# Triangular inversion of the recurrent tiles: the 4x4 blocks by a square and one product, the square copied by ScalarE

## What is computed

```
def step(state, inp):
    r_t, w_t, k_t, v_t, kk_t, a_t = inp
    sa = jnp.einsum('bhij,bhj->bhi', state, -kk_t)
    state = (state * w_t[:, :, None, :] + sa[..., None] * (kk_t * a_t)[:, :, None, :]
             + v_t[..., None] * k_t[:, :, None, :])
    return state, jnp.einsum('bhij,bhj->bhi', state, r_t)
```

## Time and profile before

| | |
|---|---|
| three runs | 1869.55, 1875.81, 1876.41 us |
| median | 1875.81 us |
| profiled execution, span from first to last instruction | 1869.1 us |
| `mix`, eight tiles | some 560 us |
| TensorE busy | 87% |
| VectorE busy | 50% |
| ScalarE busy | 30% |
| GpSimd busy | 20% |

### The profile page before, as it was taken

How to read it: one execution, slowest core, us unless ns; L and a number is a source line. 1 busy time by engine, 2 the same in 40 slices (tenths; PEclk the granted TensorE clock), 3 DMA queues, 4 the chain that set the end, 5 groups by cost and what they waited for, 6 DMA issues and landing times. The chain is left out here.

```text
span 1869.1 us, 40718 instructions
## 1 busy us (share of the span) xinstructions
PE 1629.8 (87%) x16070; PEld 1075.9 (58%) x16071; DVE 937.1 (50%) x2046; ACT 559.8 (30%) x1099; POOL 369.4 (20%) x825
## 2 busy tenths in 40 slices
PE   4999999876788889888886898498999999999976
PEld 2744444336666667676664455365666666666652
DVE  4257686346768777768562224432233333333326
ACT  4115887723334434434332112010111111111121
POOL 7301457701101100101000000111111111111110
PEclk8999999988899999999997999599999999999997
DMA  9513434320013011000002563599999799978735
GB/s 332 164 60 150 162 127 167 121 86 27 13 28 106 14 38 28 13 28 18 19 8 75 192 218 137 224 352 408 405 398 366 285 385 388 366 294 313 285 138 230
DMA packets 131649, 334.88 MB, mean 179 GB/s; under 512 B 14174, under 2 KB 52110, under 8 KB 130497
## 3 DMA queue, kind: packets, MB, share of 16 engines
q1 hardware_dynamic: 122496, 314.12, 44.6%
q0 software_dynamic: 9024, 19.00, 3.5%
HBM read 303.23 MB, written 38.82 MB: 183 GB/s over the span
## 5 line engine op out<-in xcount | busy, mean ns | idle before, releaser
L2043 PE MATMUL psX<-arena 128*64 128x256 f32 x1536 | 180.0, 388 | 14.2 <-DMA arena<-in_e_down_dram 12.6
L2067 PE MATMUL psP<-arena 128*64 128x512 f32 x768 | 175.4, 599 | 0.0
L2043 PEld LDWEIGHTS psX<-arena 128*64 128x64 f32 x1536 | 115.2, 140 | 91.4 <-issue 43.5
L806 PE MATMUL psP<-arena 128*128 128x512 f32 x320 | 141.1, 595 | 4.4 <-DVE arena L712 2.9
L506 ACT ACTIVATE arena<-arena 128x1024 bf16<-128x1024 f32 (+5 forms) x138 | 134.2, 973 | 32.5 <-POOL arena L464 28.6
L806 PE MATMUL psX<-arena 128*128 128x512 f32 x320 | 140.9, 595 | 3.4 <-DVE arena L712 1.9
L1740 PE MATMUL psP<-arena 128*128 128x512 f32 x256 | 116.4, 613 | 9.8 <-PEq L112 4.6
L1918 ACT ACTIVATE arena<-arena 64x1024 f32<-64x1024 f32 x49 | 51.7, 1055 | 237.9 <-PE psT L2029 210.9
L1927 ACT ACTIVATE arena<-psX 128x256 f32<-128x256 f32 x48 | 18.4, 383 | 317.3 <-PE psX L2043 317.3
L1261 PE MATMUL psP<-ckvT,arena 128*128 128x512 f32 (+3 forms) x192 | 79.4, 524 | 33.2 <-DVE st L1100 22.0
L806 PEld LDWEIGHTS psP<-arena 128*128 128x128 f32 x320 | 59.9, 190 | 81.4 <-issue 75.4
(11 more groups left out here) (413 smaller groups left out, 2870.0 us busy)
## 6 DMA issues: line engine op xcount, KB each, us to landing
arena<-in_e_gate_dram SPq DMA_DIRECT2D x32, 2048.0 KB, 9.5
arena<-in_e_up_dram SPq DMA_DIRECT2D x32, 2048.0 KB, 15.2
arena<-in_e_down_dram SPq DMA_DIRECT2D x32, 2048.0 KB, 9.4
arena<-in_ada_w_dram SPq DMA_DIRECT2D x12, 2048.0 KB, 16.4
proj_T<-arena SPq DMA_DIRECT2D x36, 256.0 KB, 2.0
arena<-in_x_dram SPq DMA_DIRECT2D x16, 512.0 KB, 5.7
arena<-in_w_in_dram SPq DMA_DIRECT2D x4, 2048.0 KB, 8.4
arena<-in_final_ada_w_dram SPq DMA_DIRECT2D x4, 2048.0 KB, 12.3
```

Source lines behind the costliest of these rows:

```text
L806: mm = pe.matmul(psum[b], w[:, k, first:first + P], hT[:, k, 512 * half:512 * half + 512], start=(k == 0), stop=(k == KD - 1))
L2043: mm = pe.matmul(psum["X0"][BLK * h:BLK * h + BLK, 0:DE // 2], xT[:, k, :], gate_w[u][:, k, DE // 2 * h:DE // 2 * (h + 1)], start=(k == 0) ...
L2067: mm = pe.matmul(psum["P0"][BLK * half:BLK * half + BLK, :], hidT[:, f, h, :], down_w[u][:, KE // 2 * h + f, D // 2 * half:D // 2 * (half ...
```

## The change

Level 0 and level 1 become one step on the 4x4 diagonal blocks. With N4 the part of N inside the 4x4 blocks, N4 to the fourth power is zero, so the inverse of (I - N4) is (I + N4)(I + N4 N4).

- Constants: `m_lvl[0]` becomes the upper mask of the 4x4 blocks (levels 0 and 1 added), `m_first` the lower one. Six more rows on GpSimd behind the `steps` constants.
- VectorE writes `low4` = N4 (plain) from PSUM in place of `AA`, then `high4` = N4 transposed into TT[0] with no identity, then `AA`, which is wanted from level 2 on only. The identity is added to TT[0] behind the X of level 1, where VectorE masked X before.
- TensorE makes X of level 1 from `low4` and TT[0]: the square of N4. It needs no mask, and ScalarE copies it to `Xs`. The products W and the addition L1214 stay as they are.
- GpSimd writes TT[1] with one addition, `low4` plus identity, in place of a mask and an addition.
- One more buffer, `low4`, of 512 columns.

```diff
@@ -450,6 +450,9 @@
                     step(pool.memset(halves[:, i:i + 1], -float(2.0 ** -(i + 1))))
                 for i in range(SEQ // BLK - 1):
                     step(pool.memset(steps[:, i:i + 1], float(BLK * (i + 1))))
+                step(pool.tensor_tensor(m_lvl[:, 0, :], m_lvl[:, 0, :], m_lvl[:, 1, :], ALU.add))
+                both_chunks(m_lvl[:, 1, :], lambda: merge(2, False))
+                step(pool.tensor_tensor(m_first[:, :], m_first[:, :], m_lvl[:, 1, :], ALU.add))
                 step(pool.memset(Z[:, :, :, :], 0.0))
                 pool.wait_ge(*at("kv_var", 0))
                 link(pool, pool.tensor_tensor(kv_rs, kv_var, mhalf[:, 0:2 * NT], ALU.pow), "kv_rs", 0)
@@ -849,6 +852,7 @@
             mixT, qlT, olT = A.take(KD, P), A.take(NH, P), A.take(NH, P)
             lg = A.take(2, SEQ)
             PT = A.take(NT, 2, P)
+            low4 = A.take(2, NPAIR, CHUNK)

             s_mx, s_gn, s_kk = st[:, 40:48], st[:, 48:72], st[:, 72:88]
             s_bon = (st[:, 24:32], st[:, 32:40])
@@ -943,10 +947,8 @@
                     ends = dx.rearrange("p (q c) i -> p c q i", c=2)[:, :, :, CHUNK:].to_broadcast([P, 2, NPAIR, CHUNK])
                     spread = ident64[:, :].unsqueeze(1).unsqueeze(1).to_broadcast([P, 2, NPAIR, CHUNK])
                     link(pool, pool.tensor_tensor(decI, ends, spread, ALU.mult), "dec_i", t)
-                    pool.wait_ge(*at("aa", t, 1))
-                    T0 = TT[:, :, 1, :, :]
-                    step(pool.tensor_tensor(T0, AA, m_first[:, :].unsqueeze(1).unsqueeze(1).to_broadcast([P, 2, NPAIR, CHUNK]), ALU.mult))
-                    link(pool, pool.tensor_tensor(T0, T0, spread, ALU.add), "t_first", t)
+                    pool.wait_ge(*at("low4", t, 1))
+                    link(pool, pool.tensor_tensor(TT[:, :, 1, :, :], low4, spread, ALU.add), "t_first", t)
                     if t:
                         output_roots(t - 1)
                     if t + 1 < NT:
@@ -1043,6 +1045,9 @@
                     for l in range(1, LEVELS):
                         next(turns, None)
                         if l == 1:
+                            for g in range(2):
+                                act.wait_ge(*at("x_done", t, l, g))
+                                link(act, act.activation(Xs[:, g], by_q(f"X{g}", CHUNK), ACT.Copy), "square", t, g)
                             act.wait_ge(*at("a_turned", t))
                             link(act, act.activation(R[:, :, :, 0, :], psum["T1"].rearrange("p (q g i) -> p q g i", q=NPAIR, g=2), ACT.Copy), "a_rows", t)
                             act.wait_ge(*at("av_done", t))
@@ -1186,10 +1191,11 @@
                         dve.wait_ge(*at("aa_done", t))
                         if t:
                             dve.wait_ge(*at("t_first", t - 1))
+                        link(dve, dve.tensor_tensor(low4[:, g], by_q(f"W{g}", CHUNK), each(m_first[:, :], NPAIR), ALU.mult), "low4", t, g)
+                    Tt0 = TT[:, :, 0, :, :]
+                    link(dve, dve.tensor_tensor(Tt0, AbB[:, :, :, 0, :], m_lvl[:, 0, :].unsqueeze(1).unsqueeze(1).to_broadcast([P, 2, NPAIR, CHUNK]), ALU.mult), "high4", t)
+                    for g in range(2):
                         link(dve, dve.tensor_tensor(AA[:, g], by_q(f"W{g}", CHUNK), each(m_low[:, :], NPAIR), ALU.mult), "aa", t, g)
-                    Tt0 = TT[:, :, 0, :, :]
-                    step(dve.tensor_tensor(Tt0, AbB[:, :, :, 0, :], m_lvl[:, 0, :].unsqueeze(1).unsqueeze(1).to_broadcast([P, 2, NPAIR, CHUNK]), ALU.mult))
-                    link(dve, dve.tensor_tensor(Tt0, Tt0, ident64[:, :].unsqueeze(1).unsqueeze(1).to_broadcast([P, 2, NPAIR, CHUNK]), ALU.add), "tt", t, 0)
                     if t:
                         centre(t - 1)
                     next(turns, None)
@@ -1200,9 +1206,13 @@
                     next(tail, None)
                     whole = dx[:, :, CHUNK:CHUNK + 1].to_broadcast([P, NH, CHUNK])
                     for l in range(1, LEVELS):
-                        for g in range(2):
-                            dve.wait_ge(*at("x_done", t, l, g))
-                            link(dve, dve.tensor_tensor(Xs[:, g], by_q(f"X{g}", CHUNK), each(m_lvl[:, l, :], NPAIR), ALU.mult), "xs", t, l, g)
+                        if l == 1:
+                            dve.wait_ge(*at("x_done", t, l, 1))
+                            step(dve.tensor_tensor(Tt0, Tt0, ident64[:, :].unsqueeze(1).unsqueeze(1).to_broadcast([P, 2, NPAIR, CHUNK]), ALU.add))
+                        else:
+                            for g in range(2):
+                                dve.wait_ge(*at("x_done", t, l, g))
+                                link(dve, dve.tensor_tensor(Xs[:, g], by_q(f"X{g}", CHUNK), each(m_lvl[:, l, :], NPAIR), ALU.mult), "xs", t, l, g)
                         next(turns, None)
                         if l == 1:
                             link(dve, dve.tensor_tensor(g8(hatB), by8(natB), whole, ALU.mult), "hat_b", t)
@@ -1370,12 +1380,12 @@
                             if l > 1:
                                 pe.wait_ge(*at("tt", t, l - 1, g))
                             else:
-                                pe.wait_ge(*at("tt", t, 0))
-                                pe.wait_ge(*at("aa", t, g))
-                            fill(pe, f"X{g}", "xs", t, l, g)
+                                pe.wait_ge(*at("high4", t))
+                                pe.wait_ge(*at("low4", t, g))
+                            fill(pe, f"X{g}", *(("xs", t, l, g) if l > 1 else ("square", t, g)))
                             for p in range(NPAIR):
                                 for c_ in range(2):
-                                    mm = pe.matmul(by_q(f"X{g}", CHUNK)[part(c_), p, :], AA[part(c_), g, p, :], TT[part(c_), g, 0, p, :], start=True, stop=True)
+                                    mm = pe.matmul(by_q(f"X{g}", CHUNK)[part(c_), p, :], (AA if l > 1 else low4)[part(c_), g, p, :], TT[part(c_), g, 0, p, :], start=True, stop=True)
                             mm.then_inc(*sig("x_done", t, l, g))
                         next(turns, None)
                         if l == 1:
@@ -1405,9 +1415,11 @@
                                 mm = pe.transpose(g4(psum["T0"])[:, p, :], g4(hatK)[:, p, :], ident[:, :])
                             mm.then_inc(*sig("k_turned", t))
                         for g in range(2):
-                            pe.wait_ge(*at("xs", t, l, g))
                             if l == 1:
+                                pe.wait_ge(*at("square", t, g))
                                 pe.wait_ge(*at("t_first", t))
+                            else:
+                                pe.wait_ge(*at("xs", t, l, g))
                             fill(pe, f"W{g}", "tt", t, l, g)
                             for w in range(2 if l < LEVELS - 1 else 1):
                                 for p in range(NPAIR):
```

## The result

| | before | after |
|---|---|---|
| median beside each other | 1874.34 us (5 runs) | 1856.67 us (5 runs, 1853.71 to 1863.21) |
| ratio, 95% interval | | 0.9919 [0.9903, 0.9935] |
| repeated later | 1872.09 (11), 1872.3 (13) | 1859.3 (6), 1860.19 (6); 0.9932 [0.992, 0.9945], 0.9936 [0.9921, 0.9952] |
| profiled execution, its span | | 1853.71, 1852.0 us |

The change makes the kernel 0.6 to 0.8% faster: by the three ratios 12 to 15 us, while the two medians of the first row lie 17.7 apart. The forecast was 8.6 us and 1867.2, with 1860 as its low end: the direction is right and the size too small. The three stages of the first two profiles (span 1869.1 and 1852.0) differ by 0.75 us in `project`, 13.5 in `mix` (its preparation of tile 0 and its end included, so 609 and not 560 us) and 2.8 behind it.

A forecast was written before the change was run, and what follows sets the result against it. VectorE was taken to set the pace at each tile's start, where TensorE's head 1 logits waited 22.0 us in all. Terms -7.6 + 1.8 - 2.8 = -8.6 us took 1875.8 to 1867.2 us; range 1860 to 1875.

The forecast's parts named there:

- the term for level 1: Level 1, tiles 2 to 6: GpSimd's shifted product collides with VectorE's scaling, +0.35 us on average, +1.8 us in all.
- start of the tile: VectorE's masks at each tile's start: 0.76 us less in eight tiles, 0.22 in the seven with `centre`, together -7.6 us.
- clock: TensorE's granted clock: with a third less idle time at tile starts some falls go, -2.8 us (bounds 0 and 7.8).
- tile 3's good case: Level 1 of tile 3: scaling starts early enough, and `hat_b` beats GpSimd's product, 0.75 us less; five times makes the -3.7 end.
- the five that the prediction counted: Falls of TensorE's clock in tiles 1, 2, 3, 4 and 7; -2.8 us was half of all five's expected worth.
- Rival 1: TensorE's clock stays as it is, the falls move along with the work: 1870.0 us, chance 17%.
- ScalarE and the constants: Two more ScalarE copies per tile fit its gap; eight small GpSimd instructions fit its wait: no cost.
- rival 3: ScalarE's copies come late for W, up to 0.77 us a tile, 6.2 in all: 1873.4 us, chance 8%.
- Rival 2: GpSimd's root holds VectorE at level 1, some 1.1 us more in two tiles together: 1868.3 us, chance 8%.
- Rival 4: Clock falls grow at W and X of level 1, slower than before: +10.4 us, 1880.4 us, chance 5%.

The follow-up runs named there:

- Experiment 3: Kernel before, with only VectorE's level 0 mask and identity moved ahead of the masks for `AA`, no operation removed: 1865.16 us, ratio 0.996.
- before with three: Kernel before plus three never-read 128x512 TensorE products in each tile's first wait, to hold the clock up: 1863.42 us, ratio 0.9956.
- after with two: Changed kernel plus two never-read 128x512 TensorE products in each tile's first wait: 1864.03 us, ratio 0.996.
- experiment 5: Changed kernel, with GpSimd's first product for the next tile held until VectorE has made `hat_b`: 1860.41 us, ratio 0.9937.
- experiment 4: Changed kernel, with the square copied by VectorE ahead of the identity and not by ScalarE: 1860.57 us, ratio 0.9936.
- experiment 2: Unread TensorE products of 128x512 in each tile's first wait: into before, six 1886.27 us, three 1863.42; into after, four 1864.96, two 1864.03, two without tile 0 1860.25.
- experiment 6: Changed kernel, with VectorE's `centre` of the tile before moved behind the first masked maximum: 1864.55 us, ratio 0.9957; together with the held GpSimd product 1864.14 us, 0.9955.

## Why the prediction was right in direction and too small

The step that failed is the term for level 1, forecast as +1.8 us and measured as -1.9. The terms of the sum stand below beside what the traces give: starts from all profiles of both kernels, level 1 from the pair with products, and for the clock the falls near the tiles' starts. These are the excess of each kernel, from head 0's maximum to the first addition of W, over its own version with products (in tile 0, where the products run over, over 6.19 us, its length in before), as the mean of two profiles of before and three of after:

| term | forecast | measured |
|---|---|---|
| start of the tile | -7.6 | -7.6 |
| level 1 | +1.8 | -1.9 |
| clock | -2.8 | -3.2 |
| sum | -8.6 | -12.7 |

**Start of the tile: right, to the hundredth.** 0.76 us less in tile 0 (2.40 to 1.64) and 0.98 in each of tiles 1 to 7 (4.28 to 3.30). The masks out of PSUM kept their 0.88 beside GpSimd, and TensorE's wait in tile 1 went from 3.31 to 2.33, as foreseen. Experiment 3 shows the same cause from the other side.

**Level 1: the step that failed.** The prediction let GpSimd's product for the next tile shift "by up to 0.6 us" and took from that a collision with the scaling (L1112) worth +0.35 on average in tiles 2 to 6, and nothing in tile 1. The shift itself was about right. What was not worked out tile by tile is what VectorE does at that moment. Us behind the end of L1145 (L1150), in before with three and after with two:

```
tile                        1      2      3      4      5
before: product starts    1.87   1.87   1.87   1.87   1.86
        scaling starts    1.81   1.94   2.07   2.41   2.85
        hat_b starts      2.19   3.16   3.22   3.30   3.51
after:  product starts    2.31   2.31   2.54   2.31   2.32
        scaling starts    1.62   1.74   1.94   2.40   2.87
        hat_b starts      2.00   2.20   2.46   3.73   3.81
```

In tiles 1 to 3 VectorE has now begun `hat_b` before the product starts, so it is GpSimd's product that waits (1.28, 1.49, 1.51 us against 1.04 alone) and VectorE loses nothing, where before its scaling (tiles 2 and 3) or `hat_b` (tile 1) was held up. VectorE is also 0.13 to 0.20 us earlier there, since one addition stands in place of two masks; the prediction had seen this and counted nothing. So tile 3's good case, -0.75, which the prediction kept only as an end of its range, held in tiles 1, 2 and 3 (-0.91, -1.03, -0.70). In tile 1 I had counted nothing for want of a wait: there TensorE's W was late only because of the clock. In tiles 4 and 5 the product still comes first and VectorE loses: +0.44, which was not foreseen for tile 4, and +0.28, half of the +0.64 forecast for tile 5. In tiles 2 to 6 that makes -0.20 us on average in place of +0.35.

One part of the way was wrong as well. The root L921 does not shift by the addition; it starts as early as before and becomes longer, 2.09 us where it took 1.64, which moves the product by 0.44 us. In tile 3 its end is held up too. Timelines of tile 3, VectorE and GpSimd, after:

```profile
628.07 0.69 DVE L1211 TENSOR_TENSOR arena<-arena,ident 128x512 f32<-128x512 f32 x1
...
629.99 0.49 DVE L1112 TENSOR_SCALAR arena<-arena,st 128x512 f32<-128x512 f32 x1
630.51 0.69 DVE L1218 TENSOR_TENSOR arena<-arena 128x512 f32<-128x512 f32 x1
628.18 2.34 POOL L921 TENSOR_TENSOR st<-st,mhalf 128x8 f32<-128x8 f32 x1 [6.96 <-DVE st L1150]
630.60 1.51 POOL L931 TENSOR_TENSOR arena<-arena,cols 128x512 f32<-128x512 f32 x1
```

L921 ends at 630.52, just behind the end of L1112 (630.48). With 2.09 us it would have ended at 630.27 and the product would have come ahead of `hat_b`. In tile 2 of this profile the root takes 2.23 us, again to just behind the scaling's end; in the other two profiles of the kernel after it takes 2.09 there.

That the losses in tiles 4 and 5 come from the product is shown by experiment 5. That the root is longer because of the addition beside it is borne out by experiment 4: there a copy out of PSUM stands first, and the root is back at 1.65 us and the product at 1.87. That the root's end waits for L1112 is read from where the two end and wasn't tried by itself.

**Clock: right in kind and about in size.** At the starts of the tiles the two profiles of before lose 4.7 and 6.8 us to falls, the three of after 1.5, 2.4 and 3.9. The scatter within one kernel is nearly as large as the difference, so that the -3.2 is near the forecast partly by luck. In the first profile four tiles lose something there (1, 3, 4 and 7), not the five that the prediction counted. The mean granted clock over all executions points the same way: 0.0042 more, an estimated 3.5 us by the slope of before's own runs. That falls in before cost about this much is borne out by experiment 2, where three products took them away and gained 8 us. That the shorter wait is the reason for fewer falls is not shown: experiment 6 made the wait at this place shorter still, and falls turned up behind the moved wait in tiles 1, 5 and 7. Rival 1, a clock that stays as it is, is unlikely: the first two terms alone would give a ratio of 0.9949, above two of the three intervals and inside the third.

**The number.** Of the 10.5 us between 1867.2 and 1856.67 the terms above explain some 4, and 1.5 lie in the median of before, which came out at 1874.34 and not at 1875.8. The rest is no larger than the scatter of the first five runs (1853.71 to 1863.21): the repetitions gave 1859.3 and 1860.19, at the low end of the range.

**ScalarE and the constants: no cost, as forecast.** The copies start 0.04 us behind L982 and W waits for none of them; rival 3 is refuted. Rival 2 is refuted by tile 1: L1112 kept 0.35 us at 502.35 while the root ran from 500.88 to 502.97. By the Trainium skill (SBUF — State Buffer, Who interferes with whom) the root, being first, would have had the shared ports for its whole instruction and L1112 would have waited; here the trace disagrees, and it is the root that waits. Rival 4, more falls, did not come.

**What stays open.** The sum, -12.7, lies within the three measured ratios (-12 to -15 us). Later in the tiles falls come and go from one execution to the next: from level 1 of tile 0 to the start of tile 1 the three profiles of after take 48.54, 53.83 and 47.07 us. This scatter of up to 7 us within one kernel can't be put down to an edit. Why products that hold the clock up gain 8 us before the change and nothing after it isn't settled either: in tile 0 they ran over, and without tile 0 the loss was gone, but the mean clock with them rose to 0.9524 (8 runs) without a shorter time. It also stays open whether the 9.5 us of the first two terms, read from the profiles, would be gained in full at an undisturbed clock: the two kernels with products lie only 0 to 3 us apart in time. The rival that a good part of the whole gain is regained clock, and not VectorE's time, is therefore not excluded.

## What to carry to other kernels

Before removing an operation on VectorE, look at what GpSimd does at that moment: one VectorE instruction at twice its own length beside a GpSimd one says that a reordering alone may give a good part of what a removal gives (here 7.5 of 12 to 15 us). When an edit shifts two engines against each other, work out the other engine's instructions with their own delays, instruction by instruction, before giving the collision a sign. And where TensorE waits in every tile, its idle time may be paid twice, in the wait and in the clock of what follows; give the second part its own term, from the granted clock of several executions and not of one.

## What the runs showed of the hardware

- GpSimd's root of 8 columns takes 1.64 us in level 1 where it begins beside VectorE's mask or copy out of PSUM, 2.09 when it begins beside VectorE's 512-column addition and 2.23 or 2.34 where its end also meets VectorE's scaling. VectorE's instructions beside it keep their lengths (0.35, 0.49).
- Beside GpSimd's 512-column product VectorE's addition of 512 columns takes 1.64 us for 0.69 and its scaling of 640 columns 1.30 for 0.55; with one input in PSUM it keeps its 0.88 for two.
- The lower level of TensorE's clock turned 1.15 us into 1.97 for 32 small products, and 1.96 into 3.44 for four large ones. Products that nobody reads, put into its wait, made the kernel before 8 us faster and the kernel after no faster.
- The mean granted clock of one and the same kernel lay between 0.941 and 0.950 from execution to execution, and its time follows it with 0.83 us for each 0.001.
